# Attention scores from stacked float32r halves instead of fp32, with negated logits and batched outputs, in a two-layer hybrid encoder

## What is computed

```python
h = rms_norm(x, norm_mix); qa,ka,va, qb,kb,vb, qc,kc,vc, fz = split(h @ w_in)
# q and k of every head RMS-normalised with gains; logf = log_sigmoid(fz + b_f)
A: s = q k^T/8 + rel_bias, window of 128; m = max(s.max, sink)
   p = exp(s - m) / (sum exp(s - m) + exp(sink - m));      o = p v      # 6 heads, 2 kv heads
B: p0, p1 = softmax(s0 + bias), softmax(s1 + bias)  # two maps a head, 32 wide, chunk-causal
   o = rms_norm((p0 - lam * p1) v) * (1 - lam_init)                      # 4 heads
C: p = softmax(q k^T/8 + cum_q - cum_k), causal;           o = p v      # 6 heads
x += concat(oA, oB, oC) @ w_out;   x += (silu(h w_gate) * (h w_up)) @ w_down, h = rms_norm(x)
```

## Time and profile before

| | us |
|---|---|
| median of 3 runs | 3482.25 (3479.91 to 3482.97) |
| profiled execution, device time | 3486.92 |
| its span | 3485.3 |

### The profile page before, as it was taken

The page is one execution under the profiler, slowest core; times in us unless marked ns, Lnnn a source line. Parts: engine busy times, 40 slices in busy tenths (PEclk is TensorE's granted clock), DMA queues, the critical chain, the costliest instruction groups (busy, mean ns, idle before and its releaser), DMA issues. The chain is left out here.

```text
span 3485.3 us, 50528 instructions
## 1 busy us (share of the span) xinstructions
PE 3209.2 (92%) x18146; PEld 2875.4 (83%) x18146; DVE 1688.8 (48%) x4058; ACT 1076.2 (31%) x2321; POOL 354.5 (10%) x216
## 2 busy tenths in 40 slices
PE   0699899998899999999968997999988999999999
PEld 0589777786799999999957896777778999999998
DVE  0344378644245445445445445784433454454454
ACT  1332266554231111111123225665524111111112
POOL 0222010000010100100012211010001001001000
PEclk9899899998999999999989998999999999999999
DMA  7244554333021111111024445525132111111111
GB/s 175 79 138 137 158 122 107 88 83 117 19 67 37 54 36 36 54 36 36 24 90 127 135 137 139 132 70 131 35 103 67 37 36 54 36 38 52 36 36 61
DMA packets 368395, 274.95 MB, mean 79 GB/s; under 512 B 128546, under 2 KB 336366, under 8 KB 368186
## 3 DMA queue, kind: packets, MB, share of 16 engines
q1 hardware_dynamic: 368218, 272.70, 28.0%
HBM read 195.84 MB, written 78.62 MB: 79 GB/s over the span
## 5 line engine op out<-in xcount | busy, mean ns | idle before, releaser
L1526 DVE TENSOR_TENSOR x<-x,ffn_down 128x512 f32<-128x512 f32 x792 | 509.5, 684 | 0.0
L1548 DVE TENSOR_TENSOR ffn_xn<-ffn_xn,ffn_up 128x384 f32<-128x384 f32 x132 | 73.2, 554 | 752.7 <-ACT ffn_xn L1493 752.7
L410 PE MATMUL ffn_up<-ffn_h_hi,ffn_hi_g 128*128 128x384 f32 x1056 | 355.4, 337 | 2.0 <-DVE ffn_h_lo L243 2.0
L410 PE MATMUL ffn_up<-ffn_h_hi,ffn_hi_u 128*128 128x384 f32 x1056 | 355.2, 336 | 0.0
L412 PE MATMUL ffn_up<-ffn_h_hi,ffn_lo_g 128*128 128x384 f32 x1056 | 354.8, 336 | 0.0
L412 PE MATMUL ffn_up<-ffn_h_hi,ffn_lo_u 128*128 128x384 f32 x1056 | 354.8, 336 | 0.0
L411 PE MATMUL ffn_up<-ffn_h_lo,ffn_hi_g 128*128 128x384 f32 x1056 | 354.8, 336 | 0.0
L411 PE MATMUL ffn_up<-ffn_h_lo,ffn_hi_u 128*128 128x384 f32 x1056 | 354.8, 336 | 0.0
L988 PE MATMUL att_S<-att_kT,att_qT 128*128 128x512 f32 (+3 forms) x864 | 324.1, 491 | 32.7 <-DMA att_qT<-scratch_qkT 25.7
L1493 ACT ACTIVATE ffn_xn<-ffn_up 128x384 f32<-128x384 f32 x132 | 64.9, 492 | 858.5 <-PE ffn_up L412 858.5
L410 PE MATMUL prj_acc<-prj_w_hi,prj_h_hi 128*128 128x384 f32 (+2 forms) x864 | 318.1, 368 | 0.0
(11 more groups left out here) (174 smaller groups left out, 5749.6 us busy)
## 6 DMA issues: line engine op xcount, KB each, us to landing
ffn_raw_g<-in_w_gate SPq DMA_DIRECT2D x44, 512.0 KB, 4.0
ffn_raw_u<-in_w_up SPq DMA_DIRECT2D x44, 512.0 KB, 5.1
ffn_raw_d<-in_w_down SPq DMA_DIRECT2D x44, 512.0 KB, 5.0
scratch_qkv<-prj_nat SPq DMA_DIRECT2D x72, 192.0 KB, 1.9
prj_w_raw<-in_w_in SPq DMA_DIRECT2D x64, 192.0 KB, 2.5
scratch_qkv<-prj_nat SPq DMA_DIRECT2D x36, 256.0 KB, 2.1
att_kT<-scratch_qkT SPq DMA_DIRECT2D x16, 576.0 KB
att_vn<-scratch_qkv SPq DMA_DIRECT2D x16, 576.0 KB, 8.3
```

The costliest lines, as they stand in the source:

```text
L410: pe.matmul(out, l_hi, r_hi, start=first, stop=False)
L1526: dve.tensor_tensor(x, x, down[:, (q * ND + n) % 4, :], ALU.add).then_inc(added, 1)
L1548: dve.tensor_tensor(a32[:, b, :], sg[:, b, :], up[:, b, 1, 0:384], ALU.mult).then_inc(gated, 1)
```

## The change

- Scores. The projection stores q and k transposed as float32r halves, high and low (`qk_parts`), and the samples' q also whole (`q_own`). ACT makes the high half, DVE the low one (`cut_turned`); both have two buffers. In attention `qs` holds a map's q as high over low on the partitions, `ks` holds keys as high over high and low over low (two stacks, two matmuls) in A and C, and in B all four combinations on 4 x 32 partitions (one matmul). `qT`, `kT` and the clearing of `qT` are gone. The past keys are scored in fp32 as before.
- Signs. q's gain is negated, as are bias tables and masks; DVE adds and takes a running minimum `low` (A: with -sink as start), directly usable as the bias of exp(low - s). The instructions that made `bias` are gone, and with them `cumq`.
- p. DVE writes scores into a ring of six p buffers, and exp works in place.
- Sums. `vn` has a 65th column of ones, so O carries the row sums of A and C; only B and sample units sum in exp. Four units share one PSUM bank of O, and `take_out` divides and stores four at once, one iteration later; `back` only works for B. The scaling of samples at line 1209 is gone; the division follows at the output.
- x is not held during attention: `mix` loads it again after its weights. Only v is stored in a scratch, by 64-column pieces into `vn`.
- RAW is 3. The layer loop is written out, with phases named per layer. The constants of attention are loaded ahead of the first front.

```diff
-GAINS = [("q_norm_a", 0, 6, HEAD, HEAD ** -0.5), ...
+GAINS = [("q_norm_a", 0, 6, HEAD, -HEAD ** -0.5), ...
-        with nc.Fori(0, DEPTH) as layer:
+        for layer in range(DEPTH):
             project(nc, t, k, layer)
+            x_home.close()
             attend(nc, t, k, layer)
-            mix(nc, t, k, layer)
+            seat_x(f"x{layer}")
+            mix(nc, t, k, layer, rows_of[layer])
...
-    RAW, RING = 4, 12
+    RAW, RING = 3, 12
...
-                act.activation(tT[:, m % 4, 0:n], turn[:, m % 2, 0:n], ACT.Copy).then_inc(taken_qk, 1)
+                if m >= 2:
+                    act.wait_ge(qk_stored[m % 2], 32 * (m // 2))
+                if i == TP:
...
+                    act.activation(tT_own[:, 0:n], turn[:, m % 2, 0:n], ACT.Copy).then_inc(owned_qk, 1)
+                split_hi(act, tT_hi[:, m % 2, 0:n], turn[:, m % 2, 0:n]).then_inc(raised_qk, 1)
...
+            def cut_turned(m):
...
+                dve.wait_ge(raised_qk, m + 1)
+                split_lo(dve, tT_lo[:, m % 2, 0:n], turn[:, m % 2, 0:n], tT_hi[:, m % 2, 0:n]).then_inc(cut_qk, 1)
...
+    def key_stacks(self, m):
+
+        return (m,) if self.kind == "B" else (2 * m, 2 * m + 1)
...
-                sp.dma_start(kT[:, b, :], t["qkT"][g.k_row:g.k_row + P, :]).then_inc(sem, 16)
+                low_part = N_QK * TOK
+                for m in range(g.maps):
+                    q, key = g.q_row(m) * TOK, (g.k_row + m * g.D) * TOK
+                    if kind == "B":
...
+                    else:
+                        sp.dma_start(qs[:, b, m, :].bitcast(F32), rows(t["qk_parts"], q, [[low_part, 2], [TOK, HEAD], [1, TOK]])).then_inc(sem, 16)
+                        for half in range(2):
+                            sp.dma_start(ks[:, b, 2 * m + half, :].bitcast(F32), rows(t["qk_parts"], key + half * low_part, [[0, 2], [TOK, HEAD], [1, TOK]])).then_inc(sem, 16)
...
-                if 1 <= g.index < NG - 1 and fresh(groups[g.index + 1]):
-                    pool.memset(qT[:, (g.index + 1) % 2, :, :], 0.0).then_inc(q_zeroed[(g.index + 1) % 2], 1)
...
-                            last = pe.matmul(out[:, c:c + w], q, kT[:, b, k0 + c:k0 + c + w], start=True,
-                                             stop=not (g.kind == "C" and c + w == n))
+                            for x in stacks:
+                                last = pe.matmul(out[:, c:c + w], q, ks[:, b, x, k0 + c:k0 + c + w], start=x == stacks[0],
+                                                 stop=x == stacks[-1] and not (masked and c + w == n))
...
-                    dve.tensor_tensor_reduce(s[:, job % 2, 0:n], S[:, job % 2, 0:n], extra_row, 1.0, -3e38, ALU.add, ALU.max, mx[:, one]).then_inc(biased, 1)
...
+                    dve.tensor_tensor_reduce(p[:, job % RING, 0:n], S[:, job % 2, 0:n], extra_row, 1.0, ceiling,
+                                             ALU.add, ALU.min, low[:, job:job + 1]).then_inc(biased, 1)
...
+                    dve.tensor_tensor(dst, out, inv[:, jobs].unsqueeze(2).broadcast_to([P, HALF, HEAD]), ALU.mult).then_inc(taken_out, 1)
...
+            sp.dma_start(k["x"][:, 0:TP, :], x_rows[0].rearrange("a (t p) d -> p (a t) d", p=P)).then_inc(x_in, 16)
```

More of the change, by code:

```diff
@@ L123, in _ @@
                 numbers = sorted(s.num for s in self.sems)
-                assert numbers == list(range(numbers[0], numbers[-1] + 1))
-                pool.sem_clear(range(numbers[0], numbers[-1] + 1))
+                first = numbers[0]
+                for a, b in zip(numbers, numbers[1:] + [None]):
+                    if b != a + 1:
+                        pool.sem_clear(range(first, a + 1))
+                        first = b
         self.ctx.close()
@@ L425, in stores @@
         flat = f"({shape})"
+        if first in V_AT:
+            out.append((t["v"][i * P:(i + 1) * P, V_AT[first]:V_AT[first] + count], src))
         if sample:
@@ L486, in project @@
     order = [sum(bool(NORMED[v[0]]) for v in work[:u]) for u in range(NW)]
+    b_order = [sum(bool(x) for x in NORMED[:b]) for b in range(len(IN_BLOCKS))]
     def splits_at(u):
@@ L745, in _ @@
                 finish_rows(u - 1)
+                if NORMED[work[u - 2][0]]:
+                    cut_turned(order[u - 2])
                 if u == GATES:
@@ L821, in attend @@
     NJ = jobs_to[-1]
-    mx, bias, total, inv, esink = (ph.sb(n, [P, NJ]) for n in ("mx", "bias", "total", "inv", "esink"))
+    unit_of = [u for u in range(NU) for _ in range(units[u][0].per_head)]
+    low, total, inv, esink, den = (ph.sb(n, [P, NJ]) for n in ("low", "total", "inv", "esink", "den"))
     coef = ph.sb("coef", [P, NU])
-    sink = ph.sb("sink", [P, A_HEADS])
+    sink, far_sink = ph.sb("sink", [P, A_HEADS]), ph.sb("far_sink", [P, A_HEADS])
     mask_f, mask_s = ph.sb("mask_f", [P, P]), ph.sb("mask_s", [P, P])
@@ L859, in attend @@
     weighed_to = [sum(x[0].kind == "B" for x in units[:u]) for u in range(NU + 1)]
-    sinks_to = [sum(x[0].kind == "A" for x in units[:u]) for u in range(NU + 1)]
-    n_qk = {"A": 2 + 1 + 4, "B": 4 + 1 + 4, "C": 2 + 1 + 6}
-    def fresh(g):
-        return g.index < 2 or "B" in (g.kind, groups[g.index - 2].kind)
+    parts_to = [sum(x[2] in (HALF - 1, TP - 1, TP) for x in units[:u]) for u in range(NU + 1)]
+    sunk_to = [sum(x[0].kind == "A" and x[2] in (HALF - 1, TP - 1, TP) for x in units[:u]) for u in range(NU + 1)]
+    n_qk = {"A": 4 + 4 + 2, "B": 16 + 4, "C": 4 + 6 + 2}
     def to(g, parity, count):
@@ L956, in _ @@
         def _(pool):
[L957 to L958 removed]
+            pool.memset(vn[:], 1.0).then_inc(ones_set, 1)
             for g in groups:
@@ L996, in score @@
                                       start=(c == 0), stop=(c == g.nb - 1))
-                        last = pe.matmul(out[:, g.n_past:g.n_samp], q, kT[:, b, SEQ:TOK], start=True, stop=True)
+                        for x in stacks:
+                            last = pe.matmul(out[:, g.n_past:g.n_samp], q, ks[:, b, x, SEQ:TOK], start=x == stacks[0], stop=x == stacks[-1])
                     last.then_inc(scored, 1)
@@ L1153, in _ @@
             then(dve.tensor_scalar(neg_lam[:], k["lam"][:], -1.0, None, ALU.mult))
+            then(dve.tensor_scalar(far_sink[:], sink[:], -1.0, None, ALU.mult))
             then(dve.tensor_scalar(subln[:], subln[:], keep[:, 0:1], None, ALU.mult))
@@ L1208, in back @@
-                if i == TP:
-                    dve.tensor_scalar(p[:, u % 3, 0, 0:n], p[:, u % 3, 0, 0:n], inv[:, a:a + 1], None, ALU.mult).then_inc(normed, 1)
-            def take_out(u, late):
-                g, h, i = units[u]
-                if (i == TP) != late:
-                    return
-                if h == 0 and i == 0 and g.index >= 2:
-                    dve.wait_ge(turned, place["mix", g.index - 2, 2] + 1)
-                dst = mixn[:, g.index % 2, i, h * HEAD:(h + 1) * HEAD]
-                if late:
+                then(dve.reciprocal(inv[:, a + 1:e], total[:, a + 1:e]))
@@ L1268, in mix @@
     came = [ph.sem(f"came{i}") for i in range(2)]
-    high, cut, done, added, squared = (ph.sem(n) for n in ("high", "cut", "done", "added", "squared"))
+    high, cut, done, added, squared, x_in = (ph.sem(n) for n in ("high", "cut", "done", "added", "squared", "x_in"))
     src = t["w_out"][layer]
```

317 lines of the change are left out of this document (180 added, 137 removed).

## The result

| | us |
|---|---|
| before, median of the runs beside it | 3482.22 |
| after, median of 4 runs | 4378.41 (4372.24 to 4383.13) |
| ratio after / before | 1.2574 (1.2552 to 1.2596) |
| forecast | 3389 (3338 to 3450) |

What follows compares the result with a forecast made beforehand. C bound by TensorE, B near TensorE's and VectorE's limits, A by loads and idle gaps. Per layer +4.6 - 14 - 13.6 - 22.5 + 0.5 = -45 us; doubled, with -3.5 for the boundary, -93.5: 3389 us, range 3338 to 3450.

Steps and rivals of the forecast that it cites:

- The stacks have rows of 4.6 KB, so I take 390 for them: Attention loads: stacks move at 390 GB/s, so the first matmul comes at 424 us instead of 416.5.
- rival (a): A groups: loads bind all of A, stacks too at 220 GB/s, B0 ends 31 us later a layer: 3451; chance 0.15.
- hidden: B and C groups: they last longer than their 5 to 8 MB of loads need, so loading costs nothing.
- B0 starts there instead of 502.4: Start of B0: near 490 us, then TensorE waits 12 us for past keys; B0 ends at 557 instead of 571.1.
- RAW 3: +2.6 and +2: Projection: three raw slots delay gain loads (+2.6 us) and the fourth slice at block ends (+2); together +4.6, bounds 0 and +10.
- Scores, C: C groups, bound by TensorE: 0.105 us less a tile, 72 tiles, -7.5 us a group, -22.5 for three.
- Rival (d): Scores on narrow pieces: float32r at 128 and 256 columns pays fp32's time, C loses 1.9 a group: about 3415; chance 0.05.
- B1: Second B group: VectorE becomes last, 58.5 us, -13.6 us; VectorE over 85% busy, TensorE near 75%.
- rival (b): B groups: VectorE and TensorE stay coupled, only bias instructions saved, 17 us less gain a layer: 3423; chance 0.10.
- Rival (c), the clock: A and B: granted clock may fall to 1.2 GHz for good, B groups +33 and +30, A +48: 3611; chance 0.07.
- The collision: Start of A2 and B0: POOL's 3.94 us clear beside VectorE's 2.59 us scaling, TensorE idling 3.11 us; both instructions go.
- Mix: Mix stage: reloading x takes 11.4 us plus 2, landing at 874.5 before the first addition at 879.3: free, 4.8 us of cover.

Runs made afterwards that it cites:

- keep_even: keep with B's stack loads writing every second of all 128 partitions instead of 64 in a row: 3379.88 us, ratio 0.9702.
- spread: Changed kernel with rows first and the two halves or copies second in attention's stack loads: 3456.02 us, ratio 0.9925 to before.
- b2_two: Kernel before, kT loaded map by map, kT and qT rows even first, then odd (first dimension 2, can't be joined): 3591.98 us, ratio 1.0302.
- b2_sixteen: Kernel before, kT loaded map by map, every sixteenth row of kT and qT first (first dimension 16): 3486.99 us, ratio 1.0003.
- vpair: Changed kernel with both faults mended, plus v of both heads in one load of 512-byte pieces instead of two of 256: 3407.78 us, ratio 0.9778.
- keep: vpair with A1 and A2 using the key stacks, v, past keys and past values loaded for A0: 3392.86 us, ratio 0.9741.
- b_raw3: Kernel before with RAW 3 instead of 4 in the projection, nothing else: 3523.54 us, ratio 1.0112.
- b_two: Kernel before with kT and qT loads written as two adjacent blocks of rows (first dimension 2): 3484.69 us, ratio 1.0000.
- b_four: Kernel before with kT and qT loads written as four adjacent blocks of rows (first dimension 4): 3485.05 us, ratio 1.0005.

## Point by point: where the prediction was wrong, and where right

The forecast, rivals (a) to (d) and the whole range failed by one term: the rate of the stacks. Times in us, layer 0, groups by the clears of qpast; spread_raw4 is the changed kernel without its two faults, the slow patterns and the missing slot.

| step | before | forecast | after | spread_raw4 | keep_even |
|---|---|---|---|---|---|
| project | 327.4 | 332 | 348.8 | 329.8 | 327.1 |
| start of attention to first score | 8.5 | 16 | 75.9 | 16.7 | 16.4 |
| A1 | 25.9 | 21.5 | 80.1 | 22.3 | 21.9 |
| A2 | 32.9 | 22 | 89.3 | 29.3 | 21.9 |
| B0 | 68.7 | 67 | 142.9 | 71.1 | 61.0 |
| B1 | 72.2 | 58.5 | 135.5 | 68.7 | 62.0 |
| C1 | 55.0 | 47.5 | 91.2 | 47.5 | 47.5 |

- **"The stacks have rows of 4.6 KB, so I take 390 for them": the step that failed.** Measured 52 GB/s. I took the rate from row length alone, and bounded it by the rates of other row lengths (220 in rival (a)); the real cause, the order of dimensions in the pattern, stood in the diff and in no row of before, where every such load begins with its rows. Rival (a) had the right direction and a bound four times too high. The price at the measured rate, six stacks of 11.1 us a front in A and C, and sixteen half stacks of 5.4 in B, is 67 us a group in A and C (whose work is 22 to 53 us) and 87 in B (61 to 71): so every group waits, and the forecast of B and C as "hidden" fell with it. The runs spread and b2_two to b2_sixteen show it. The 220 that I took for the 256-byte pieces of v and cache stood in no row of before; pieces of 256 bytes of v cost 1 to 2 us a layer before B1 (vpair).
- **390 for B, too, was wrong once that was mended:** 214 to 222 GB/s onto 64 partitions in a row; 403 to 409 onto every second of 128 (keep, keep_even). I had forecast 12 us of waiting, all for the past keys in the third unit; in spread_raw4 it was 11.3 for the front and 5.8 for the past keys. "B0 starts there instead of 502.4" failed: A2 was scored at 499.5 and B0's first score came at 511.4, 490 in the forecast. A2 itself took 29.3 us for 22: TensorE waits 2.7 us in it for A2's past keys, and the granted clock is 0.66, 0.50 and 0.56 in the 12 us from 474 to 486. The forecast had neither.
- **RAW 3: +2.6 and +2, in truth +21.** b_raw3 gives the whole of it. I costed the gain loads and one burst a block; the waits of TensorE are nine, and nearly half of the price is slower matmuls, with the granted clock lower, which I had not counted at all.
- **Scores, C: right in size.** C1 55.0 to 47.5 us, -7.5 as worked out, in every kernel with mended loads but the two with SP's queue reordered (51 to 53). The scores of eight tiles, from their start to the start of the mask's matmul, take 1.01 us in spread_raw4 and took 1.77: 0.095 us a tile where I had 0.105, so a part of the 7.5 comes from elsewhere. Rival (d) failed, but my column rate for narrow pieces was too good as well: two tiles in A, from the start of the scores to the start of the transposes, go from 0.49 to 0.33 us, and the forecast needs 0.28. A unit is 0.19 us shorter instead of 0.21, and A1 takes 21.9 to 22.3 us where 21.5 was forecast.
- **B1: nearly.** 61.0 to 62.0 in most runs, 58.5 forecast, so rival (b) is out: it had only the bias instructions, 5.5 us, going. VectorE's busy time in B1 is 52.3 us in spread for 61.2 before, -9 as forecast (my terms add up to 49.3 there, where I wrote 49.5). But it is not alone at its limit: TensorE is 88% busy, where I had near 75%. It waits 6.8 us for VectorE (4.3 of it for the weighing), and VectorE 7.9 us for TensorE's scores.
- **Rival (c), the clock: in part.** The granted clock in B1 was 0.92 instead of 1.00 in most runs, and 0.80 in one; in B0, with its waits, 0.80 to 0.89. The two B1, spread first, then spread_raw4:

```profile
608.00:618.00 10.00, 7.27 (x34) 5.91 (x34) 9.79 (x18) 7.03 (x14) 0.00 (x0) 0.71 0.48 145
618.00:628.00 10.00, 9.39 (x56) 8.20 (x56) 7.68 (x20) 6.78 (x15) 0.00 (x0) 0.78 0.94 352
628.00:638.00 10.00, 9.53 (x87) 8.29 (x86) 7.21 (x26) 6.61 (x23) 0.00 (x0) 1.00 1.05 229
```

```profile
590.00:600.00 10.00, 6.97 (x38) 5.32 (x38) 9.79 (x18) 7.04 (x13) 0.00 (x0) 0.83 0.46 137
600.00:610.00 10.00, 7.86 (x45) 7.29 (x44) 7.99 (x20) 6.42 (x14) 0.00 (x0) 0.75 0.92 348
610.00:620.00 10.00, 10.00 (x51) 9.56 (x50) 3.04 (x14) 4.14 (x15) 0.00 (x0) 0.50 0.87 189
620.00:630.00 10.00, 10.00 (x59) 9.04 (x58) 7.02 (x22) 4.89 (x14) 0.00 (x0) 0.56 0.35 55
```

  In and behind a stretch in which VectorE is full and TensorE about 70% busy (7.27 and 6.97 of 10 us), the clock goes to the lower of its two levels. In spread it is back at 1.00 from 628 on. In spread_raw4 it is low for over 20 us, with TensorE 100% busy there: the group takes 7 us more than in layer 1 of the same run. No run shows what makes the difference. So the fall exists, at about a quarter of the 30 us priced for B1 and not "for good".
- **The collision went** as forecast: no 2.59 us instruction of VectorE remains where A2 and B0 begin; in spread VectorE has none above 0.5 us from 484 to 500, where A2 begins, nor from 519 to 530, where B0 begins.
- **Mix: the price right, the cover not.** From its first load to the first up-projection matmul of feed it is 128.3 us before, 129.2 in spread, so loading x again costs 0.9 at most. But x did not land early: in spread it is issued at 846.6 and the first addition at 864.4 waits for it (9.3 us of idle VectorE, ended by that DMA), 17.8 us where 13.4 were forecast. The 4.8 us of cover are not there. **Layer boundary:** -5.2, forecast -3.5.
- **Sum.** 3389 was forecast. With the two faults mended the kernel takes 3423; the 34 us over the forecast lie in A2 (7 in layer 0), B0 (4) and B1 (10 in layer 0, 3 in layer 1). With the loads of A kept and B's spread it takes 3380, but that is a kernel with fewer loads than the one forecast, and its nearness to 3389 says nothing for the forecast. As written, 4378.

## What to carry to other kernels

Read the pattern of each DMA, not only the length of its runs: put the rows first, and a copy or a high/low dimension of 2 second. A share of 0.13 of 16 DMA engines in a stretch where everyone waits for loads is the sign of it. Then look at which partitions the load writes, and at every instruction that a load moved up in a queue has passed. Before a buffer is taken from a ring to make room, try it alone: one slot cost 40 us here.

## What the runs showed of the hardware that I had not expected

- At a DMA share of 0.13, two of 16 engines, the loads move at 52 GB/s; first dimensions of 2, 4 and 16 over the same bytes cost +105, +35 and 0 us on the kernel before. A first dimension over adjacent blocks costs nothing (b_two, b_four).
- Loads onto 64 partitions in a row moved at 214 to 222 GB/s with the DMA share at 1.03; the same bytes onto every second of 128 partitions at 403 to 409.
- Short waits of TensorE (2.1 us at most) come with nearly as much again: 10.9 us of waits and 9.1 of slower matmuls, at a granted clock of 0.97 instead of 0.99, in one projection. In A2 of spread_raw4 the granted clock is 0.50 and 0.56 from 478 to 486, behind one wait of 2.7 us.
